# One decoder step on one core: heads issued two deep, and the first query product by column blocks

## The reference

```python
s = einsum('bhtd,bhsd->bhts', q, k) * exp(dmat - m_t)
num = w_inter * einsum('bhtd,bhde->bhte', q, C) + einsum('bhts,bhse->bhte', s, v)
den = w_inter * einsum('bhtd,bhd->bht', q, n) + sum(s, -1)
h = num / maximum(abs(den), exp(-m_t))
C_new = a * C + einsum('bhs,bhsd,bhse->bhde', wk, k, v)
hm = h * rsqrt(mean(h * h) + EPS) * mh_g * sigmoid(mo)
```

## Time and profile before

| | us |
|---|---|
| median of 3 runs (2499.58 to 2512.24) | 2510.61 |
| the profiled execution | 2507.47 |
| its span | 2505.7 |
| TensorE busy | 2154.6 (86%) |
| VectorE busy | 1516.5 (61%) |
| ScalarE busy | 458.8 (18%) |
| GpSimd busy | 377.3 (15%) |
| DMA moved | 845.89 MB, 338 GB/s over the span |

### The profile page before, as it was taken

The page is one execution under the profiler, slowest core; times in us unless marked ns, Lnnn a source line. Parts: engine busy times, 40 slices in busy tenths (PEclk is TensorE's granted clock), DMA queues, the critical chain, the costliest instruction groups (busy, mean ns, idle before and its releaser), DMA issues.

```text
span 2505.7 us, 20801 instructions
## 1 busy us (share of the span) xinstructions
PE 2154.6 (86%) x7662; PEld 1204.6 (48%) x7662; DVE 1516.5 (61%) x2686; ACT 458.8 (18%) x880; POOL 377.3 (15%) x363
## 2 busy tenths in 40 slices
PE   6999999987888999989999988777777877877776
PEld 5999999855575343434444443322232322222221
DVE  4434543485485666675444568888888755555555
ACT  3323332324363001121000112111111100100001
POOL 0000000100000212111121212212222222222221
PEclk9999999999899999999999999999999999999999
DMA  6544444323987999999999999999999999999997
GB/s 185 163 134 135 135 145 154 117 91 97 340 351 300 423 425 379 422 386 426 425 417 423 399 428 409 417 414 412 409 405 411 415 428 429 428 429 428 427 429 314
DMA packets 155534, 845.89 MB, mean 338 GB/s; under 512 B 9350, under 2 KB 97218, under 8 KB 108762
## 3 DMA queue, kind: packets, MB, share of 16 engines
q0 software_dynamic: 46080, 671.11, 63.5%
q1 hardware_dynamic: 109354, 173.45, 20.0%
HBM read 834.31 MB, written 10.21 MB: 337 GB/s over the span
## 4 chain that ended last, share of the span: by engine, by line
PE 53%; DMA 32%; DVE 9%; issue 4%; ACT 1%; SPq 0%; POOL 0%; DVEq 0%; POOLq 0%
DMA rows_in<-in_peer_uv,expert 30%; PE bank L277 20%; PE bank L359 7%; PE bank L1180 6%; PE bank L1181 6%; PE bank L1182 6%; DVE rows_in L662 3%; PE bank L1158 1%; DVE diag L636 1%; PE bank L324 1%; DMA wf<-in_w_out 1%; PE bank L326 1%; PE bank L325 1%; PE bank L1260 1%; PE bank L1349 1%
## 5 line engine op out<-in xcount | busy, mean ns | idle before, releaser
L277 PE MATMUL bank<-rows_in,diag 128*128 128x512 f32 (+1 forms) x2560 | 1190.7, 612 | 262.4 <-DVE diag L636 262.2
L662 DVE CUSTOM_DVE_ANT_0 rows_in<-rows_in,x2n 128x2048 f32<-128x2048 f32 x320 | 733.6, 2292 | 532.2 <-DMA rows_in<-in_peer_uv,expert 531.9
L277 PEld LDWEIGHTS bank<-rows_in,diag 128*128 128x128 f32 (+1 forms) x2560 | 452.9, 183 | 982.4 <-issue 545.4
L567 POOL DMA_INDIRECT rows_in<-in_peer_uv,expert x320 | 365.7, 1143 | 1455.2 <-PE bank L277 1306.2
L449 ACT ACTIVATE dots<-dots 128x1 f32<-128x1 f32 x320 | 65.0, 203 | 1515.3 <-DVE dots L662 1515.3
L1180 PE MATMUL bank<-xnh,wh 128*128 128x336 f32 (+2 forms) x928 | 295.3, 318 | 4.7 <-DVE wl L1606 4.7
L1181 PE MATMUL bank<-xnl,wh 128*128 128x336 f32 (+2 forms) x928 | 291.6, 314 | 0.0
L1182 PE MATMUL bank<-xnh,wl 128*128 128x336 f32 (+2 forms) x928 | 291.5, 314 | 0.0
L1606 DVE TENSOR_TENSOR wl<-wring,wh 128x2048 fp32r<-128x2048 f32 (+1 forms) x58 | 132.1, 2279 | 211.4 <-ACT wh L1413 211.4
L1180 PEld LDWEIGHTS bank<-xnh,wh 128*128 128x128 f32 (+1 forms) x928 | 174.9, 188 | 12.4 <-issue 11.1
L1181 PEld LDWEIGHTS bank<-xnl,wh 128*128 128x128 f32 (+1 forms) x928 | 175.0, 189 | 1.3
(11 more groups left out here) (303 smaller groups left out, 1381.5 us busy)
## 6 DMA issues: line engine op xcount, KB each, us to landing
wring<-in_w_in SPq DMA_DIRECT2D x28, 2048.0 KB, 8.3
wf<-in_w_out SPq DMA_DIRECT2D x16, 1024.0 KB, 8.8
wf<-in_peer_wq SPq DMA_DIRECT2D x16, 1024.0 KB, 6.5
wk<-in_w_out SPq DMA_DIRECT2D x32, 512.0 KB, 11.2
wk<-in_peer_wq SPq DMA_DIRECT2D x32, 512.0 KB, 10.4
kT<-in_keys_t SPq DMA_DIRECT2D x16, 512.0 KB, 5.8
vpage<-in_cache_v SPq DMA_DIRECT2D x16, 512.0 KB, 6.2
rows_in<-in_peer_uv,expert POOLq DMA_INDIRECT x320, 12.5
```

Source lines behind the costliest of these rows:

```text
L277: mm = pe.matmul(accs[t][d][0:w, :], diag[r % ND][:, 0:w], rows_in[r % NG][:, D + 512 * d:D + 512 * d + 512], start=False, stop=(j == ROUN ...
L567: nc.gpsimd.indirect_dma_start(out=rows_in[r % NG][:], out_offset=None, in_=UV_DR, in_offset=bass.IndirectOffsetOnAxis(ap=ids[:, j:j + 1], ...
L662: nc.vector.tensor_tensor_reduce(u, u, x2n[t][:], 1.0, 0.0, ALU.mult, ALU.add, dots[t % 2][:, j:j + 1]).then_inc(S["dot_done"], 1)
```

## The change

**Heads.** The jobs of the heads get banks by hand, and the decay and score cells (`mR`, `mS`) of head h+2 are issued ahead of the sample state products of head h; those of heads 0 and 1 lie between the transposes of stage 2. The cells above the diagonal that are zero are left out: 256 + 160 + 32 columns for the prompt and 64 for the samples share one bank of 512, so one decay addition, one gate in two pieces. The transposes of head h's output come behind the numerators of head h+1. The exponential takes the column term as its bias. `kw` is made by ScalarE, `kwz` by GpSimd (both halves of the partitions, four samples each), the squares by ScalarE straight from the bank. The samples' numerators and state products are split in two halves: output rows 0 to 31 and 32 to 63, and weight rows 0 to 63 and 64 to 127. The gain `mh_g` is multiplied into the gate in stage 1 (tiles 48 to 55), and the products with the gate become one operation for 512 columns.

**First query product.** `peer_wq` is loaded by column blocks: four loads of 1 MB for each block of 512 columns (runs of 2 KB), and TensorE does one block's 48 matmuls and closes its bank before the next. The queries of block d-1 lie between the units of block d. Buffers: `wf` has six up to load 23 and three from load 24 on; `wfh` three from load 16 on. Head 0's expert selection is done by VectorE in three pieces behind the low parts 23, 24 and 25, and GpSimd issues four gathers as soon as it is done (the last two when block 1's bank is closed).

The diff, cut to its core:

```diff
@@ plan_jobs
+    jobs += [(("sW",), 4)] + cells(0)
+    jobs += [(("nat", i, q), free[(5 * i + q + 1) % 5]) for i in range(4) for q in range(2, 7)]
+    jobs += [(("n0",), 5), (("bs",), 6)]
+    jobs += cells(1)
     for h in range(MH):
-        jobs += [("mR", h)] + [("mS", h, j) for j in range(3)]
-        jobs += [("sR", h), ("sW", h), ("sS", h)]
-        jobs += [("mN", h, 0), ("mN", h, 1), ("mC", h), ("sN", h), ("mT", h, 0), ("mT", h, 1)]
+        jobs += [(("mN", h, 0), 2), (("mN", h, 1), 3)]
+        jobs += turns(h - 1) if h else []
+        jobs += [(("mC", h), 4), (("sN", h), 5)]
+        jobs += cells(h + 2) if h + 2 < MH else []
+        jobs += [(("sC", h, n * SB // 2 + p), (6, 7, 4)[(2 * p + n) % 3]) for p in range(SB // 2) for n in range(2)]
@@ buffers
+    def slot_of(n):
+        return n % NF if n < FEW else n % (NF // 2)
+    def high_slot(n):
+        return n % NH if n < KC else n % (NH - 1)
+        def column_blocks():
+            for n in range(KC, 2 * KC):
+                d, k = (n - KC) // KU, (n - KC) % KU
+                slot_ready(n)
+                src = a["peer_wq"][0][KU * P * k:KU * P * (k + 1), 512 * d:512 * d + 512].rearrange("(k p) c -> p k c", p=P)
...
@@ tail_tensor
+            for d in range(4):
+                n = KC + KU * d
+                unit(n)
+                if d:
+                    query(0, d - 1, "qt")
+                unit(n + 1)
+                if d == 1:
+                    pe.wait_ge(S["keys_in"], 16)
+                if d:
+                    query(0, d - 1, "pS")
+                for k in range(2, KU):
+                    unit(n + k)
+            query(0, 3, "qt")
+            query(0, 3, "pS")
@@ tail_pool
-        take(pool, ("wq", 0, 3))
+                if r == NG // 2:
+                    full_read(pool, FEW - 1)
@@ tail_vector
                 for n in range(KC + 5, 2 * KC):
                     weight_low(dve, n)
+                    for u in range(HSTEPS)[2 * (n - KC - 7):2 * (n - KC - 6)] if n >= KC + 7 else ():
+                        head_step(0, 0, u)
@@ tensor, heads
+                halves_ = [b[TS // 2 * n:TS // 2 * n + TS // 2, 0:DV + 1] for n in range(2)]
+                for q in range(SB // 2):
+                    for n in range(2):
+                        pe.matmul(halves_[n], wide[:, at_:at_ + TS // 2], C0[s][:, n * SB // 2 + q, :], start=(q == 0), stop=False, skip_group_check=True)
...
+                for p in range(SB // 2):
+                    for n in range(2):
+                        half = slice(TS * n, TS * n + TS)
+                        close(pe.matmul(b[:, 0:DV + 1], kwz[s][half, p, :], mv_nat[half, 3, h, :], start=True, stop=True))
@@ vector, heads
             for h in range(MH):
+                normalizer(h, 0, ecol[:, 0:2, h], P, (0, 1), [take(dve, ("mN", h, i)) for i in range(2)])
+                if h + 1 < MH:
+                    head_gate(h + 1)
                 if h:
+                    mix_in(h - 1)
+                normalizer(h, 2, ecol[0:TS, 2:3, h], TS, (2,), [take(dve, ("sN", h))])
+                if h + 2 < MH:
+                    head_decay(h + 2)
+                for p in range(SB // 4):
+                    states(h, p)
+                head_norm(h)
+                for p in range(SB // 4, SB // 2):
+                    states(h, p)
```

561 lines of the change are left out of this document (334 added, 227 removed).

## The result

The changed kernel takes 2533.39 us, median of 11 runs, against 2512.17 us for 11 runs of the kernel before. The ratio is 1.0101, 95% interval [1.0084, 1.0118], so it is slower, by 21 us at the medians. The forecast was 2507, range 2487 to 2522. The profiled execution has a span of 2529.6 us, 23.9 more than the one of before.

A forecast was written before the change was run, and what follows sets the result against it. Gathers of expert rows were taken to bound a fixed-length block, so its start counted. Heads -10.4 and first query product +8 gave -2.4, counted from 2509 us: forecast 2507, range 2487 to 2522.

The forecast's parts named there:

- Selection and ring (a, b): First query product: selection between low parts closes the last bank at 789, with three buffers at 793.5, against 781.2.
- Gathers beside the loads (c): End of first query product: gathers share DMA with the last loads, 7.2 us a load; last bank 798.6 instead of 793.5.
- The cutting into 2 KB: First query product's loads: 2 KB runs as fast as 8 KB, up to 0.2 us a load for the range.
- Heads: the low clock goes away: Head stage: no low clock in the heads as a sign of being right; gain 10.4 us, bounds 5.5 to 14.
- Column groups: Heads' sample numerators: ten at 0.46 us, no overlap; the rival that they overlap gave 2500 us, chance 0.06.
- my path of a head: TensorE's steps in a steady head: 11.6 us, then the sample updates with their waits, 15.8 us in all.
- Loads behind the product: From last bank to the block: loads of 3.5 MB no longer meet fresh gathers, 12 us instead of 13.8.
- Early rows bring 7 us: Block: rows landed early save waits between 795 and 910 and part of those at 941; 7 us, between 4 and 14.
- The signs listed: Trace marks of being right: gathers issued near 758, block's first matmul near 801, first logit about 10 us earlier.
- signs of being wrong: Last bank under 8 us later, head period under 14 or over 17 us, or 950 to 1434 waits falling over 5.
- -10.4 + 8: Whole kernel: heads gain 10.4 us, first query product with early rows costs 8; -2.4 in sum.
- three-buffer ring becomes the bound: First query product: every round from unit 24 on takes 14.4 us plus low clock; 2521 us, chance 0.15.

The follow-up runs named there:

- e1_late: Changed kernel with the first gathers held until the first query product's last bank closes; ratio 1.0088 to the kernel before.
- e3_nosel: e1_late with six weight buffers to the product's end and head 0's selection behind the product, as in the kernel before; one execution, 2507.8 us.
- e6_landed: Changed kernel with the four gathers held until the first query product's last weight load has landed; ratio 1.0164 to the kernel before.
- e5_rows8k: Changed kernel with the first query product's 16 loads reading whole rows in 8 KB pieces instead of 2 KB; 2534.5 us, ratio 1.0119.
- h4_fill_all: h2_fill with the same extra matmuls also in waits of head 3 and the start-up; 2495.63 us, ratio 0.9949 to the kernel before.
- h2_fill: New heads with the old first query product, plus three extra matmuls ahead of the last two sample updates in heads 0 to 2; 2498.67 us.
- e2_six: e1_late with six weight buffers, and four for their high parts, to the end of the first query product; one execution, 2532.5 us.
- b1_fill: Kernel before with five extra matmuls ahead of each head's numerators, nothing reordered; 2511.13 us, ratio 1.0019.
- c1_groups: h2_fill with the eight sample numerators as four on one 32-column group, then four on the other, not by turns; one execution, 2497.9 us.

## Why the prediction was wrong, point by point

**Selection and ring (a, b).** Right in mechanism and nearly in size: 12.3 forecast; 12.1 measured (e1_late against the kernel before), or 10.5 against e3_nosel, of which 3.9 by the ring and 6.6 by the selection.

**Gathers beside the loads (c).** The step that failed. I had 5.1 us, and 1 for the clock; it is 20.5 (79.8 less 59.3), or 14.8 measured from e6_landed's 65.0. A part of it is the clock: from 795.5 us to the close, with the last loads there, it was 0.73, which is 4.2 us by the arithmetic above, where I had 1. I let the loads share DMA evenly, 7.2 us for each, and followed the units by that. The queues share by packet, and the loads had 2 KB against 16. Yet e5_rows8k shows that even sharing would not have saved the sum: a third of the bytes for the loads leaves 16.8 of the 20.5. The sum that I needed is one line: 8.4 MB of gathers at 0.42 MB a microsecond are 20 us, the last three loads come behind or among them, and with three buffers TensorE has nothing else to do. I had the figure 31 us for 13.4 MB in the text and did not draw the conclusion that the last load lands at its end.

**The cutting into 2 KB.** I said "I take them at the same speed". Alone they nearly are (the last three of e1_late land in 4.9 to 5.0 us, the least before is 4.8). Against another queue they are not.

**Heads: the low clock goes away.** The other step that failed. I expected the clock to rise as the waits of 2.5 us became shorter; the waits became 1.25 us, and the clock fell more, from 0.93 to 0.83 over the heads. With the clock held at 1.00 every forecast stretch of the heads comes out within 0.8 us (h4_fill_all). The sum of the work came out right, and its clock was assumed. Why the clock falls is shown in part only: filling the waits brought it back in heads 1 to 3 of h2_fill, but head 0 of e2_six and the attention in b1_fill ran at half speed with TensorE busy in nearly all of the time.

**Column groups.** Misread. The earlier trace rows has eight matmuls of 32 columns in 3.73 us, and I read 0.46 each as the full price. The granted clock of that stretch, which I had not read, is the third number from the end here:

```profile
634.90:638.60 3.70, 3.70 (x18) 1.48 (x17) 1.67 (x1) 0.27 (x1) 0.00 (x0) 0.50 0.97 274
```

At 0.50, 3.73 us is two at a time at half speed. In the changed kernel the same kind of row is 1.93 us at 1.00. The rule of the Trainium skill that I set aside (TensorE: Matmul & The Clock Gate, Part 3: Packing small matmuls) holds here. It takes 2.2 us off my path of a head (4.6 forecast, 2.4 measured in h4_fill_all), and c1_groups shows that the period follows this time one for one. Yet the period is 15.6 us against my 15.8, because other terms were too small: numerators 2.8 and not 2.3, the state 1.7 and not 1.4, the sample updates with their waits 5.3 (5.1 in the changed kernel) and not 4.2. So the 10.4 us, which h4_fill_all nearly gives, is in part luck: errors of opposite sign stand inside it.

**Loads behind the product.** 12 us forecast without fresh gathers, 14.1 measured; in the kernel before, with four gathers beside the end of it, it was 13.8. So the gathers cost nothing there, and the 2 us that I took off for them were wrong.

**Early rows bring 7 us.** 6.1 measured in the block (1710.5 less 1704.4), from one execution of each. 3.9 of them come from the place I named, the first 115 us, where TensorE is busy 114.8 us instead of 110.9. The 6 us at 941 did not move:

```profile
825.00:940.00 115.00, 114.77 (x261) 50.71 (x262) 67.66 (x137) 9.40 (x26) 23.11 (x18) 0.97 0.92 373
940.00:980.00 40.00, 33.94 (x73) 14.49 (x72) 27.22 (x51) 6.86 (x19) 5.95 (x5) 0.91 0.96 404
```

The three kernels whose four gathers are issued before the product's last load need 1711.8 to 1722.3 us from the last bank to the end, the eight with the old order of gathers and loads 1720.8 to 1731.4; the means are 8.8 apart. So the rows bring some 6 to 9 us, and no place was found where they cost less.

**The signs listed.** The gathers went out at 766.0, not near 758; but that is 34.7 us into the product, and the forecast of 769 in the clock of before is 34.8. The selection was timed rightly, and the 8 us are the heads' gain that did not come, less the 3 us of the projection. The block's first matmul came at 825.2, not 801; the row of low parts waiting on high parts that wait for DMA is there (units 29 to 31), and no wait on rows 2 or 3 shows in the first 115 us of the block. Of the signs of being wrong one came, by a hair: the second head took 17.0 us, from 517.19 to 534.21, the others 15.4 and 15.0. TensorE's waits of the 484 us from 950 (980 in the changed kernel) went from 16.1 to 15.2 us, so the ring sets them, as I had said.

**Sum and rivals.** -10.4 + 8 became +0.2 + 26.8 (32.6 + 0.3 - 6.1). The rival *three-buffer ring becomes the bound* had the sign and the place (loads beside the gathers, loads past 9 us), with half of the price; I gave it 0.15 because the row for DMA at 1.01 seemed to be about another stage. It is the same resource. The slower case should have had the larger chance and no upper end at 22 us.

## What to carry to other kernels

Before a bulk transfer is moved ahead into a stage with idle DMA, divide its bytes by the rate and ask what that stage still has to load: with few buffers, the stage is longer by most of the quotient (14.8 to 20.5 of 20 us here). Compare the packet sizes of the two queues, since small pieces get the smaller share, and look for an operation that happens to delay the bulk transfer now. Read the granted clock of every row that a price is taken from, and where TensorE waits a little in each round, put work of another step, or even empty matmuls, in the wait and measure.

## What the runs showed of the hardware

- Two DMA queues were served packet for packet, by the records of the profile: 154 to 158 with packets of 16 and 2 KB (88.6% of the engines' time for the one), 109 to 116 with 16 and 8 KB (two thirds).
- The same head code took 15.4 us or 24.3 us, with TensorE busy in over nine tenths of it, at a granted clock of 0.95 or 0.50. A whole head in e2_six (its one wait 0.72 us), and 33 us of attention in b1_fill (TensorE busy 32.3 of them), ran at 1.2 GHz without a long wait in them. Adding 1.3 us of matmuls to each of three waits took the ratio from 1.0002 to 0.9975. The Trainium skill (TensorE: Matmul & The Clock Gate, A second HAM failure mode: psum-queue depth-cycling) describes a kernel whose clock swings because TensorE idles briefly between groups while it goes round its banks; the waits of 1.25 us for a bank, and what filling them did in h2_fill, agree. The two stretches just named, busy throughout, it doesn't explain.
- Matmuls on two groups of 32 columns ran side by side: eight of 257 columns in 1.93 us by turns, 2.83 us in two blocks of four, both at a clock of 1.00.
